# A delta rule with 32-square diagonal blocks inverted on VectorE, and a memory attention whose shares are scaled on ScalarE, inside a four-layer network kernel

## The reference, cut to what matters

```python
G = jnp.cumsum(gc, axis=-1)
diff = G[..., :, None] - G[..., None, :]
decay = jnp.where(incl, jnp.exp(jnp.where(incl, diff, 0.0)), 0.0)
kk = jnp.einsum("bhnid,bhnjd->bhnij", kc, kc)
lower = jnp.where(strict, bc[..., :, None] * kk * decay, 0.0)
rhs = jnp.concatenate([vc * bc[..., None], kc * (bc * jnp.exp(G))[..., None]], axis=-1)
sol = lax.linalg.triangular_solve(lower + jnp.eye(CHUNK, dtype=f32), rhs, left_side=True,
                                  lower=True, unit_diagonal=True)
u, w = sol[..., :GDN_DV], sol[..., GDN_DV:]
p = jnp.einsum("bhnid,bhnjd->bhnij", qc, kc) * decay
def step(state, xs):
    u_n, w_n, qg_n, kg_n, p_n, gl_n = xs
    v_new = u_n - jnp.einsum("bhcd,bhde->bhce", w_n, state)
    o_n = jnp.einsum("bhcd,bhde->bhce", qg_n, state) + jnp.einsum("bhij,bhje->bhie", p_n, v_new)
    state = state * gl_n[..., None, None] + jnp.einsum("bhcd,bhce->bhde", kg_n, v_new)
    return state, o_n
o = rms_norm(o, out_norm) * jax.nn.silu(split_heads(z, GDN_HEADS).astype(jnp.float32))
p = jax.nn.softmax(s, axis=-1)
y = jnp.concatenate([y_mix, y_mem], axis=-1) @ w_out[layer]
```

## Time and profile before

| what | value |
| --- | --- |
| median of 3 runs | 2255.43 us (2255.23 to 2260.67) |
| the profiled execution, its own time | 2260.27 us |
| its span, first to last instruction | 2258.5 us |
| TensorE busy | 2065.9 us, 91% |
| VectorE, ScalarE, GpSimd busy | 1154.8, 756.2, 144.0 us |
| mean granted clock of TensorE | 0.958 |

### The profile page before, as it was taken

How to read it: one execution, slowest core, us unless ns; L and a number is a source line. 1 busy time by engine, 2 the same in 40 slices (tenths; PEclk the granted TensorE clock), 3 DMA queues, 4 the chain that set the end, 5 groups by cost and what they waited for, 6 DMA issues and landing times.

```text
span 2258.5 us, 30595 instructions
## 1 busy us (share of the span) xinstructions
PE 2065.9 (91%) x11940; PEld 1786.9 (79%) x11940; DVE 1154.8 (51%) x1605; ACT 756.2 (33%) x1154; POOL 144.0 (6%) x140
## 2 busy tenths in 40 slices
PE   7999656899999987999999999988999789999996
PEld 7888556899999986888888787768888567888884
DVE  4633576254434449544445688446666434333344
ACT  4442333142322333422324333653322433222221
POOL 0100344000000000000000000001111111000000
PEclk9999787999999999999999999999999899999998
DMA  4211000222222222222232222210000122223221
GB/s 163 71 52 38 29 0 0 84 85 87 92 86 94 85 84 84 94 93 95 95 99 94 75 93 93 75 38 1 0 0 0 38 75 75 93 85 103 97 86 50
DMA packets 43385, 156.94 MB, mean 69 GB/s; under 512 B 4816, under 2 KB 5072, under 8 KB 43152
## 3 DMA queue, kind: packets, MB, share of 16 engines
q1 hardware_dynamic: 43136, 154.40, 20.8%
q10 hardware_dynamic: 144, 1.05, 0.1%
HBM read 153.33 MB, written 2.10 MB: 69 GB/s over the span
## 4 chain that ended last, share of the span: by engine, by line
PE 84%; DVE 8%; ACT 3%; DVEq 2%; issue 2%; DMA 0%; ACTq 0%; SPq 0%; POOL 0%
PE ps L442 69%; PE ps L853 7%; PE ps L564 1%; PE ps L732 1%; DVEq L1637 1%; PE ps L813 1%; PE ps L705 1%; DVE XE L1633 1%; DVE wlo L1469 1%; DVE W L1779 1%; PE ps L703 1%; DVE GT L1987 0%; DMA raw<-W 0%; DVEq L1927 0%; PE ps L485 0%
## 5 line engine op out<-in xcount | busy, mean ns | idle before, releaser
L442 PE MATMUL ps<-UH,whi 128*128 128x264 f32 (+1 forms) x1952 | 677.5, 347 | 39.2 <-issue 15.3
L442 PE MATMUL ps<-UL,whi 128*128 128x264 f32 (+1 forms) x1952 | 670.3, 343 | 0.4 <-issue 0.4
L442 PE MATMUL ps<-UH,wlo 128*128 128x264 f32 (+1 forms) x1952 | 667.7, 342 | 0.0
L986 ACT ACTIVATE whi<-raw 128x1024 fp32r<-128x1024 f32 x284 | 298.1, 1054 | 469.4 <-PE ps L442 465.7
L442 PEld LDWEIGHTS ps<-UH,whi 128*128 128x128 f32 x1952 | 373.8, 192 | 95.5 <-issue 17.6
L442 PEld LDWEIGHTS ps<-UL,whi 128*128 128x128 f32 x1952 | 373.8, 191 | 44.5 <-issue 1.9
L442 PEld LDWEIGHTS ps<-UH,wlo 128*128 128x128 f32 x1952 | 372.9, 191 | 42.6 <-issue 0.5
L1469 DVE TENSOR_TENSOR wlo<-raw,whi 128x1024 fp32r<-128x1024 f32 x284 | 345.9, 1220 | 58.5 <-ACT whi L986 58.5
L442 PE MATMUL ps<-HH,whi 128*128 128x264 f32 (+1 forms) x768 | 246.4, 321 | 0.0
L442 PE MATMUL ps<-HL,whi 128*128 128x264 f32 (+1 forms) x768 | 246.3, 321 | 0.0
L442 PE MATMUL ps<-HH,wlo 128*128 128x264 f32 (+1 forms) x768 | 245.7, 320 | 0.0
(11 more groups left out here) (341 smaller groups left out, 2582.8 us busy)
## 6 DMA issues: line engine op xcount, KB each, us to landing
raw<-W SPq DMA_DIRECT2D x284, 512.0 KB, 3.4
H<-xT SPq DMA_DIRECT2D x4, 528.0 KB, 7.3
out<-H SPq DMA_DIRECT2D x8, 256.0 KB, 2.0
MEM<-memT ACTq DMA_DIRECT2D x1, 1024.0 KB, 4.8
masks<-masks SPq DMA_DIRECT2D x1, 768.0 KB, 10.2
TAB<-rope SPq DMA_DIRECT2D x1, 264.0 KB, 13.2
vecs<-vecs SPq DMA_DIRECT2D x1, 101.0 KB, 3.5
ABW<-gates SPq DMA_DIRECT2D x1, 64.0 KB, 12.8
```

The lines of the kernel that those rows point to most:

```text
L442: mm = pe.matmul(dst, a, b, start=start and n == 0, stop=stop_ and n == 2)
L986: act.activation(whi[s % NB][:, :, :], raw[s % NB][:, :, :], ACT.Copy).then_inc(w_hi, 1)
```

## The change

The chunk loop goes. Four things take its place, all unrolled.

First, for all chunks at once, TensorE makes the cumulated gates with the causal mask already added (a product of the identity with the mask `future`, -1e30 above the diagonal, and four products with `upper`), ScalarE turns them into decays (`PTD`) with the gate as bias, TensorE multiplies keys by keys, and VectorE multiplies the two into `WU`. The factor beta is moved into the exponent.

Second, the four diagonal blocks of 32 of all 32 matrices (4 chunks, 8 heads) are moved by VectorE's 32-square transposes to one array `LD` of 32 x 32 positions for each partition, and 31 steps of forward substitution invert them all together: a multiplication and a subtraction, with a drain before each. Two more transposes give the inverse and its transpose. The steps stand in VectorE's queue between the maxima (`top`) and reciprocals (`share`) of memory attention. The shares are scaled by ScalarE, the values are transposed beside that.

Third, TensorE joins the 32-blocks to 64 and the 64-blocks to 128, with products of 64 or 32 columns (`corner32`, `update32`, `corner64`, `update64`): chunks 0 and 1 before the loop, chunks 2 and 3 inside it.

Fourth, an unrolled loop over the chunks does the products with the state, the solution, the new state and the outputs. The norm moves in: ScalarE squares with a sum by row, VectorE scales, TensorE turns, VectorE gates, ScalarE and VectorE split into `YH` and `YL`. The work space is the memory of the weights' halves, so the first slots of the output projection are converted only at the end of the loop. The projection takes the memory attention's four blocks first. GpSimd only zeroes. Masks, counters of semaphores and helper arguments are adapted.

The core of the diff; `-` lines of the old loop are named above and left out:

```diff
@@ TensorE
+            def decay(j):
+                if j >= 2:
+                    pe.wait_ge(G["dec"], j - 1)
+                b = j % 2
+                pe.matmul(ps[:, b, :].rearrange("p (x t) -> p x t", x=4), ident,
+                          future.rearrange("p (a t) -> p a t", a=1).to_broadcast([P, 4, P]), start=True, stop=False,
+                          skip_group_check=True)
+                for x in range(4):
+                    mm = pe.matmul(ps[:, b, x * P:(x + 1) * P], SCAL[:, 0, 4 * j + x:4 * j + x + 1].to_broadcast([P, P]),
+                                   upper, start=False, stop=True, skip_group_check=True)
+                mm.then_inc(G["gb"], 1)
+            for j in range(8):
+                decay(j)
+                keys(j)
...
+            def update32(c):
+                b, p = 2 * (c % 2) if c < 2 else 0, c % 2
+                pe.wait_ge(G["ac"], levels_done(c, 32))
+                for h in range(GH):
+                    pe.matmul(ps[:, b, 32 * h:32 * h + 32], WU[:, 8 * c + h, :], A32[p][:, h, 0:32], start=True, stop=True)
+                for h in range(GH):
+                    w = WU[:, 8 * c + h, :].rearrange("p (a b t) -> p a b t", a=2, b=2)
+                    mm = pe.matmul(ps[:, b + 1, 64 * h:64 * h + 64].rearrange("p (a t) -> p a t", a=2), A32[p][:, h, :],
+                                   w[:, :, 1, :], start=True, stop=True)
+                mm.then_inc(G["p"], 1)
...
+            for part in (corner32, update32, corner64, update64):
+                part(0)
+                part(1)
...
+            for c in range(4):
+                if c:
+                    state_products(c, 0)
+                    state_products(c, 1)
+                if c + 2 < 4:
+                    corner32(c + 2)
+                solved(c, 0)
+                solved(c, 1)
+                if c:
+                    outputs_turned(c - 1, 0)
+                if c + 2 < 4:
+                    update32(c + 2)
+                outer(c, 0)
+                outer(c, 1)
+                if c:
+                    outputs_turned(c - 1, 1)
+                for n in ((0, 1, 2, 3), (4, 5, 6, 7), (8, 9), ())[c]:
+                    if n % 2 == 0 and c + 2 < 4 and n in (2, 6):
+                        corner64(c + 2)
+                    piece(n)
+                if c + 2 < 4:
+                    update64(c + 2)
+            outputs_turned(3, 0)
+            outputs_turned(3, 1)
@@ ScalarE
+            def shares(h):
+                act.wait_ge(M["x"], 2 * HEADS + h + 1)
+                for c in range(4):
+                    a = am_p[h % 2][:, c, :]
+                    last = act.activation(a, a, ACT.Copy, scale=am_s[h % 2][:, 12 + c:13 + c])
+                last.then_inc(M["p"], 1)
...
+            for c in range(4):
+                if c:
+                    queries_out(c, 0)
+                    queries_out(c, 1)
+                if c + 2 < 4:
+                    base(c + 2)
+                solved(c, 0)
+                solved(c, 1)
+                if c + 2 < 4:
+                    corner32(c + 2)
+                if c:
+                    gated_hi(c - 1, 0)
+                if c == 0:
+                    keys_out(2, 3)
+                if c == 1:
+                    keys_out(4, 3)
+                rstd_heads(c, 0)
+                rstd_heads(c, 1)
+                if c:
+                    gated_hi(c - 1, 1)
+                if c + 2 < 4:
+                    corner64(c + 2)
+                if c == 0:
+                    keys_out(3, 3)
+                if c == 1:
+                    keys_out(5, 3)
+                if c == 3:
+                    weights_hi(0, to=BLOCK0["wout2"] // SLOT + 2)
+            gated_hi(3, 0)
+            gated_hi(3, 1)
+            weights_hi(0, to=BLOCK0["wout2"] // SLOT + 4)
@@ VectorE
-                dve.tensor_tensor(a[:, :, :], a[:, :, :],
-                                  b[:, 12:16].rearrange("p (c k) -> p c k", k=1).to_broadcast([P, 4, NMEM]), ALU.mult
-                                  ).then_inc(M["p"], 1)
+            def eliminate(first, last):
+
+                for s in range(first, last):
+                    m, w = 31 - s, s + 1
+                    a = prod[:, 0:m * w].rearrange("p (t j) -> p t j", j=w)
+                    x = XI[:, s + 1:32, 0:w]
+                    dve.drain()
+                    dve.tensor_tensor(a, XI[:, s:s + 1, 0:w].to_broadcast([P, m, w]),
+                                      LD[:, s + 1:32, s:s + 1].to_broadcast([P, m, w]), ALU.mult)
+                    dve.drain()
+                    dve.tensor_tensor(x, x, a, ALU.subtract)
+            for q in range(4):
+                a = 32 * q
+                dve.transpose(LD[a:a + 32, :, :], WU[a:a + 32, :, a:a + 32].rearrange("p n t -> p t n"))
+            top(0)
+            top(1)
+            dve.wait_ge(G["clear"], 1)
+            eliminate(0, 5)
+            share(0)
+            eliminate(5, 8)
+            share(1)
+            eliminate(8, 14)
+            top(2)
+            eliminate(14, 20)
+            share(2)
+            top(3)
+            eliminate(20, 25)
+            share(3)
+            eliminate(25, 31)
+            dve.drain()
+            dve.transpose(TDG[:, :, :], XI[:, :, :].rearrange("p t s -> p s t"))
+            dve.transpose(UDG[:, :, :], XI[:, :, :]).then_inc(G["inv"], 1)
```

More of the change, by code:

```diff
@@ L226, in build @@
+        GT = [GT0, GT1]
         FH, FL, FO, GA0, GA1, GS0, GS1, GC0, GC1 = region(
@@ L835, in _, with memory_values, values_turned @@
                 mm.then_inc(M["t"], 1)
+            def memory_values(h):
+                pe.wait_ge(M["tc"], UNITS + h + 1)
+                if h:
+                    pe.wait_ge(N["ma_end"], h)
+                for x in range(2):
+                    mm = pe.matmul(ps[:, 4, :], VMT[:, x, h * P:(h + 1) * P], am_t[:, x, :], start=x == 0, stop=x == 1)
+                mm.then_inc(N["ma_o"], 1)
+            def values_turned(j):
+                c, g = j // 2, j % 2
+                if j >= 2:
+                    pe.wait_ge(G["vtc"], j - 1 if j < 4 else j)
+                turned(4 + j % 2 if j < 4 else 5, lambda x: chunk(16 + 4 * g + x, c)).then_inc(G["vt"], 1)
@@ new lines, in keys_turned, with queries @@
+            def keys_turned(j, bank):
+                c, g = j // 2, j % 2
+                turned(bank, lambda x: chunk(8 + 4 * g + x, c)).then_inc(G["kt"], 1)
+            def queries(j, bank):
+                c, g = j // 2, j % 2
+                four(bank, lambda x: chunk(8 + 4 * g + x, c), lambda x: chunk(4 * g + x, c)).then_inc(G["kq"], 1)
+            pe.wait_ge(G["dec"], 8)
+            scores(0)
+            pe.wait_ge(G["w"], 8)
+            scores(1)
+            for j in range(4):
+                values_turned(j)
@@ L914, in _ @@
[L914 to L922 removed]
+                values_turned(4 + h)
+                if h == 0:
+                    pe.wait_ge(G["vtc"], 3)
@@ new lines, in solved @@
+            def solved(c, g):
+                pe.wait_ge(G["up"], levels_done(c, 64))
+                if c:
+                    pe.wait_ge(G["r"], 2 * (c - 1) + g + 1)
+                elif g == 0:
+                    pe.wait_ge(N["ma_end"], HEADS)
+                    pe.wait_ge(M["tc"], UNITS + HEADS)
+                r = (lambda x: RR[g][:, x, :]) if c else (lambda x: chunk(16 + 4 * g + x, 0))
+                four(4 + 2 * g, lambda x: WU[:, 8 * c + 4 * g + x, :], r).then_inc(G["y"], 1)
@@ new lines, in _ @@
+            for j in range(8):
+                decay(j)
+            for j in range(4):
+                values_out(j)
+            exps(0)
+            exps(1)
+            shares(0)
+            shares(1)
+            shares_out(0)
+            values_out(4)
+            memory_out(0)
+            exps(2)
+            shares_out(1)
+            shares(2)
+            values_out(5)
+            memory_out(1)
+            exps(3)
+            shares_out(2)
+            shares(3)
+            values_out(6)
@@ new lines, in _, with residual @@
+            update32(0)
+            update32(1)
+            update64(0)
+            update64(1)
+            def residual(c, g):
+                dve.wait_ge(G["ks"], 2 * (c - 1) + g + 1)
+                for x in range(4):
+                    n = 8 * c + 4 * g + x
+                    last = dve.scalar_tensor_tensor(RR[g][:, x, :], ps[:, 4 + 2 * g, x * P:(x + 1) * P], SCAL[:, 1, n:n + 1],
+                                                    QKV[:, 16 + 4 * g + x, c * P:(c + 1) * P], ALU.mult, ALU.add)
+                last.then_inc(G["r"], 1)
```

681 lines of the change are left out of this document (354 added, 327 removed).

## The result

The changed kernel takes 2189.55 us (median of 4, 2184.99 to 2192.68), the kernel before in the same runs 2258.05: the ratio is 0.969 [0.967, 0.972]. It is faster, as forecast, but by 68.5 us and not by 103.6, and it lies 10.6 us above the range's upper end. The profiled execution took 2192.68 us, 67.6 less than the one before. First the page of the changed kernel, which answers to the earlier trace rows.

What follows compares the result with a forecast made beforehand. The limit was a ping-pong of small products, copies and subtractions per chunk in a 288.4 us stretch. Steps (a) to (d), 176.7, plus 8.1 for the clock gave 184.8, 103.6 less: 2152 us, range 2139 to 2179.

Steps and rivals of the forecast that it cites:

- (a): Start of the new stretch: decays and key products for all chunks, 24.2 us.
- (b): VectorE's elimination, transposes and memory attention work, then ScalarE's remainder and chunk 0's diagonal blocks: 44.7 us.
- (c): Joining the blocks for chunks 0 and 1: 2 x 40 products at 0.223 us and 1.4 of waits, 19.3 us.
- (d): The loop over four chunks with its tail: TensorE's products, transposes and waits, 88.5 us.
- (e): TensorE's clock in the new stretch: three falls behind gaps, 2.7 us each, charged as 8.1 us.
- Rival 2: Low clock stays through (c) and (d) because TensorE works in short bursts; 77 us would double: 2221 us, chance 0.06.
- The old passes kept 0.94: Argument against Rival 2: the old chunk passes, also of short groups, kept 0.94 of the clock.
- rival 1: Dearer VectorE steps: 7.6 us more for the elimination's instructions, 8 for the transposes; 2167 us, chance 0.15.
- rival 3: No fall of the clock in the new stretch, waits as written: 2144 us, chance 0.12.
- rival 4: Engine queues lock each other, so the stretch takes 301 us against 288.4: 2268 us, chance 0.03.
- rival 5: The inversion stays on the path for each chunk: about 2255 us, chance 0.01.
- the prediction's own signs of being wrong: Small instructions over 0.3 us apart, transposes above 1.3, clock near 0.5 in (c) or (d), stretch outside 175 to 205.

Runs made afterwards that it cites:

- run 11: run 10 with TensorE's long waits filled with products that nobody reads: 2149.65 us, 0.952 of the kernel before.
- run 2: The changed kernel with join products of 128 columns instead of 32 or 64: 2168.92 us, 0.962 of the kernel before.
- run 4: The changed kernel with memory attention's shares scaled by VectorE again instead of ScalarE: 2192.38 us, 0.973 of the kernel before.
- run 12: run 11 with the narrow joins of 64 and 32 columns again: 2171.24 us, 0.963 of the kernel before.
- run 10: run 8 with the four diagonal-block copies for chunks 2 and 3 moved from ScalarE to VectorE: 2157.29 us, 0.955 of the kernel before.
- run 8: run 2 with chunks 0 and 1's diagonal copies on VectorE, memory attention's split behind ScalarE's own copies, 64-row corner copy ahead of the squares: 2158.97 us.

## Why the prediction was wrong

The stretch by the forecast's steps; run 11 stands beside, because there the clock is at its upper level from the first join on:

| step | forecast | change | run 2 | run 11 |
| --- | --- | --- | --- | --- |
| (a) + (b), to the first join | 68.9 | 76.3 | 76.3 | 71.6 |
| (c), joins of chunks 0, 1 | 19.3 | 36.9 | 25.5 | 21.1 |
| (d), loop | 88.5 | 108.3 | 100.9 | 90.2 |
| (e), clock | 8.1 | in (c), (d) | in (c), (d) | 0 |
| sum | 184.8 | 221.5 | 202.7 | 182.9 |

The step that failed first of all is the clock in (c) to (e): one price for each product, at the high clock, and three falls of 2.7 us. The others that failed are the size of the transposes and of the first copies in (b), and a wait for the later copies that no step has.

**(a)** held: 24.65 for 24.2.

**(b)** missed 7.4 (with (a)). The elimination, the doubtful term, was right to 0.1 us; its fixed part behind a drain is what the earlier trace rows show. What failed is "I take 1.13" for all six transposes: the six take 7.80 + 1.99 + 1.21 = 11.0, 4.2 more. I had the bound (2.45), but took the end for neighbours where the code reads with a step. The second term is the "2.5 for the diagonal blocks of chunk 0": eight copies at 0.63 are 5.1, 2.6 more, for the same reason. The order of ScalarE's queue was right: it was free 3.4 us after VectorE (4.1 forecast). The shares on ScalarE: run 4 agrees with step (b).

**(c)** is where most was lost, 17.6. The price 0.223 for "the new products of 32 and 64 columns" came from products of 16 columns and is right (2.0 for 8 of them at the high clock); what failed is the clock assumed with it, and step (e)'s premise that a fall costs 2.7 us and then is over, taken from a recovery in 512-column products. Behind the fall came 80 products of 64 and 32 columns, and through these the clock stayed at 0.50; it is even lost without a wait (run 12). 11.4 of the 17.6 come back with wide products. Of the other 6.2, 4.2 is the wait for chunk 2's diagonal copies, which step (d) had not listed at all: with those of the next blocks they take 4.3 and 2.6 us on ScalarE, and the forecast had no wait for them. Most of the rest is the first join at the low clock, 1.6.

**(d) and (e)** together missed 11.7; 7.4 of it is again the narrow products. The waits forecast for ScalarE's squares (3.9, 3.6, 3.8) measured 3.84, 3.37 and, in chunk 2 by way of VectorE, 3.40; the tail's 5.5 and 3.1 measured 5.23 and 2.51. With the clock held, the loop takes 90.2 against 88.5 in run 11. That its sum comes so near is in part luck, since run 11 has other queues (a corner's copy put forward, copies on VectorE, filled waits) and wide joins.

So of the 36.7 us, 18.8 are the clock behind narrow products (shown by runs 2 and 12), 4.2 the transposes and 2.6 the first copies (read from rows, not taken away by a run of their own). The remaining 11.1 are the wait for the later diagonal copies (4.0; run 10 removed it) and 7.1 that were not taken apart: waits of under 1.5 us each, and perhaps, which no run shows, what the clock lost behind waits over the 8.1 charged.

**The rivals.** Rival 2 (2221, chance 0.06) named the right thing, a low clock through (c) and (d), with the wrong cause: pauses between short groups. In run 12 TensorE paused nowhere in the 27.4 us at 0.51. "The old passes kept 0.94" was no evidence against it, since all of their products had 128 columns. It held for (c) fully and for (d) in part, so the time came out about half way to it. Of rival 1 the transposes came true with 4.2 of its 8 us, the steps not at all. Rivals 3, 4 and 5 did not occur: the clock fell, the queues overlap as written, and the inversion left the path. Of the prediction's own signs of being wrong three came: transposes above 1.3 us, a clock near 0.5 in (c), and a stretch over 205 us.

## What to carry to other kernels

Price a run of small products twice, at each level of the clock, and look for a row of the same number of columns with its granted clock before taking the high one; where groups of products of 32 or 64 columns stood on the path, moving 128 cost next to nothing and brought 18.8 of 221.5 us here. Price a copy or transpose by a row with the same step between elements, not only of the same size. And once the long work is gone, ask which copies stand last in the queue of the engine that feeds the next product: eight of them given to an idle engine, four others put behind the rest and one put forward were worth 10.6 us here.

## What the hardware did that I had not expected

- The granted clock fell from 1.00 to 0.50 without a wait over 1.3 us, while TensorE did one short product after the other (run 12: eight in 2.00 at 1564.66, in 3.68 at 1567.28). It was back at 1.00 after 27.4 us of them, from 1594.70 on, fell twice more among the next joins (3.42 at 1598.05, 3.66 at 1605.06), and rose behind products of 128 columns (eight records in 1.06 from 1611.66 on). The change shows the same fall at 1611.32.
- A full-precision product takes 0.22 us at the high clock for 16, 32, 64 or 128 columns, so the wide ones cost nothing here. Only the 64-row ones were shorter when narrow: eight took 1.15 us (run 12), with 128 columns 1.86 (run 8).
- On ScalarE a step of 128 or 512 B, on either side, makes 256 elements 0.63 instead of 0.38 us, and 512 elements 1.07 instead of 0.60. VectorE makes the same copies of 512 elements in 0.60 and those of 256 in 0.54 (run 11), where 256 elements from PSUM without a step take it 0.42; why the smaller ones gain so little is not shown. Its transposes pay, 1.99 for 1.21.
